# Token-major router logits, shorter VectorE routing chain, and what fills TensorE meanwhile, in a two-block transformer kernel on one core

## What is computed

```python
h2 = rmsnorm_2(x, norm2_w[layer])
x = x + hier_moe(h2, ...)            # 4 groups x 8 experts

p_group = softmax(x32 @ wg + bg)
pg, g_sel = lax.top_k(p_group, 1)
e_in = take_along_axis(e_logits, g_sel)[:, 0]
top_v, top_i = lax.top_k(e_in, 2)
gates = softmax(top_v) * pg
ids = g_sel * 8 + top_i
order = argsort(ids);  xs = xf[order // 2];  sizes = bincount(ids)
hg, hu = ragged_dot(xs, w_gate, sizes), ragged_dot(xs, w_up, sizes)
ys = ragged_dot(silu(hg) * hu, w_down, sizes) * gates
y = segment_sum(ys, tok)
```

## Time and profile before

| | |
|---|---|
| median of 3 runs | 1033.57 us (1033.43 to 1033.9) |
| profiled execution | 1033.82 us, span 1031.9 us |
| PE busy | 1010.1 us (98%), 5626 records |
| weight loads busy (PEld) | 873.2 us (85%) |
| DVE busy | 846.8 us (82%) |
| ACT busy | 706.1 us (68%) |
| DMA queues | 253.59 MB, mean 246 GB/s |
| granted clock | 0.998 of full speed |

### The profile page before, as it was taken

How to read it: one execution, slowest core, us unless ns; L and a number is a source line. 1 busy time by engine, 2 the same in 40 slices (tenths; PEclk the granted TensorE clock), 3 DMA queues, 4 the chain that set the end, 5 groups by cost and what they waited for, 6 DMA issues and landing times.

```text
span 1031.9 us, 15025 instructions
## 1 busy us (share of the span) xinstructions
PE 1010.1 (98%) x5626; PEld 873.2 (85%) x5626; DVE 846.8 (82%) x1044; ACT 706.1 (68%) x859; POOL 40.8 (4%) x44
## 2 busy tenths in 40 slices
PE   7999999999999999999999999999999999999997
PEld 6788999999989888999878788888888888888885
DVE  5855876766677877898869799999999999999987
ACT  5664655555565756576454688888888888888874
POOL 2001000000000110101020100000000000000000
PEclk9999999999999999999999999999999999999999
DMA  9734447474725455352215899999999999999971
GB/s 344 276 123 143 164 165 235 138 236 139 231 83 169 163 166 167 123 164 83 82 34 204 325 362 372 368 367 364 383 354 375 365 374 360 384 364 373 364 300 44
DMA packets 82709, 253.59 MB, mean 246 GB/s; under 512 B 4160, under 2 KB 42176, under 8 KB 62656
## 3 DMA queue, kind: packets, MB, share of 16 engines
q1 hardware_dynamic: 82624, 252.50, 67.9%
HBM read 251.44 MB, written 1.05 MB: 245 GB/s over the span
## 4 chain that ended last, share of the span: by engine, by line
PE 42%; DVE 3%; ACT 2%; issue 2%; DMA 1%; DVEq 0%; POOLq 0%; POOL 0%; ACTq 0%
PE bank L2020 13%; PE bank L2022 13%; PE bank L2021 13%; PE bank L2521 1%; DMA raw<-in_exp_w_down 1%; DVE WL L1080 1%; PE bank L2561 1%; ACT WH L541 1%; PE bank L2480 0%; PE bank L2489 0%; ACT MXH L923 0%; DVE MXL L1627 0%; PE bank L2593 0%; PE bank L2594 0%; ACT CV L918 0%
## 5 line engine op out<-in xcount | busy, mean ns | idle before, releaser
L1080 DVE TENSOR_TENSOR WL<-raw,WH 128x2048 fp32r<-128x2048 f32 x230 | 524.5, 2302 | 89.7 <-ACT WH L541 86.6
L541 ACT ACTIVATE WH<-raw 128x2048 fp32r<-128x2048 f32 x231 | 440.6, 1914 | 83.9 <-PE bank L2022 72.3
L2020 PE MATMUL bank<-WH,MXH 128*128 128x512 f32 x552 | 218.1, 395 | 0.7 <-DVE WL L1080 0.6
L2021 PE MATMUL bank<-WL,MXH 128*128 128x512 f32 x552 | 215.2, 390 | 0.0
L2022 PE MATMUL bank<-WH,MXL 128*128 128x512 f32 x552 | 215.2, 390 | 0.0
L2020 PE MATMUL bank<-HTH,WH 128*128 128x256 f32 x576 | 165.0, 286 | 1.2 <-DVE HTL L1103 1.2
L2021 PE MATMUL bank<-HTL,WH 128*128 128x256 f32 x576 | 162.9, 283 | 0.0
L2022 PE MATMUL bank<-HTH,WL 128*128 128x256 f32 x576 | 162.9, 283 | 0.0
L2020 PE MATMUL bank<-WH,HTH 128*128 128x512 f32 x400 | 159.6, 399 | 2.1 <-DVE WL L1127 1.0
L2021 PE MATMUL bank<-WL,HTH 128*128 128x512 f32 x400 | 155.8, 390 | 0.0
L2020 PEld LDWEIGHTS bank<-WH,MXH 128*128 128x128 f32 x552 | 103.7, 188 | 29.6 <-issue 8.5
(11 more groups left out here) (411 smaller groups left out, 1079.1 us busy)
## 6 DMA issues: line engine op xcount, KB each, us to landing
raw<-in_exp_w_up SPq DMA_DIRECT2D x52, 1024.0 KB, 7.4
raw<-in_exp_w_gate SPq DMA_DIRECT2D x52, 1024.0 KB, 7.4
raw<-in_exp_w_down SPq DMA_DIRECT2D x52, 1024.0 KB, 7.3
raw<-in_w_in SPq DMA_DIRECT2D x34, 1024.0 KB, 5.3
raw<-in_w_up SPq DMA_DIRECT2D x22, 1024.0 KB, 5.3
raw<-in_w_down SPq DMA_DIRECT2D x11, 1024.0 KB, 5.2
raw<-in_w_out SPq DMA_DIRECT2D x8, 1024.0 KB, 5.1
raw<-in_w_o SPq DMA_DIRECT2D x4, 1024.0 KB, 5.7
```

What stands on the lines that cost most here:

```text
L541: e.activation(WH[i % HL][:, :], raw[i % RAW][:, :], ACT.Copy).then_inc(a_wh, 1)
L1080: e.tensor_tensor(l, r, h.bitcast(F32), ALU.subtract).then_inc(v_wl, 1)
L2020: e.matmul(out_, ah, bh, start=start, stop=False, skip_group_check=skip)
L2021: e.matmul(out_, ah, bl, start=False, stop=False, skip_group_check=skip)
```

## The change

All in the stage between the last projection and the first unit.

- **Logits.** The transposed X stays float32 in the buffer BIG, one eviction each: three by ScalarE, the last by VectorE. It is now the stationary operand, and the 36 unsplit router columns move: 4 products for each part (c, t), into one bank for each token tile (`LGB`). The router's split, the low parts, ScalarE's eviction and `small_turn` are gone.
- **Best two.** Two instructions MAX and two MAX_INDEX give the eight largest of `el` and their places; one cast adds 100, and two comparisons with the codes give the one-hots.
- **Counts.** TensorE sums both token tiles in PSUM (32 columns), and adds tile 0's counts to tile 1's ranks. VectorE's prefix sum reads PSUM.
- **Tiles.** A round is one instruction with an accumulator output (`next_limit`), with three masks ready ahead; `first` counts the experts whose prefix sum is zero.
- **Slots.** `place(t)`: two multiply-and-reduce instructions for each token tile, right ahead of that tile's SEL.
- **Order.** `rows_low(1, 0)` goes behind the routing's sum MM, `rows_low(1, 1)` behind the first half of SEL; TensorE waits for each token tile's low rows apart. ScalarE's `rows_high(1, 0)` goes ahead of two evictions. The mean is one instruction behind the squares.
- **Filling.** `warm` 20 and 36 become 13 and 18.
- **ScalarE** splits piece NP+3 behind its gathered rows, no longer ahead of them.

```diff
-        xcols = [[v[PI["we", 1, 0] % HL][:, 0:4 * S].rearrange("p (k s) -> p k s", k=4) for v in (WH, WL)],
-                 [v[:, 0:4, :] for v in (HTH, HTL)]]
+        xcols = [big(1024 * c, 4, S) for c in range(2)]
...
-            e.activation(wsh[:, 0:288], wr_norm, ACT.Copy).then_inc(a_whs, 1)
...
             x_columns(0, 1)
             half_squares(1, 0)
+            rows_high(1, 0)
             x_columns(1, 0)
-            x_columns(1, 1)
             half_squares(1, 1)
-            rows_high(1, 0)
             rows_high(1, 1)
-            e.wait_ge(p_sp, 2)
-            e.activation(TMP[0:36, 1, 0:256], bank[4][0:36, 0:256], ACT.Copy).then_inc(a_sptv, 1)
...
             split(NP + 2)
-            split(NP + 3)
...
             for k in range(0, 8, 2):
                 gathered(k, 1)
+            split(NP + 3)
...
-            e.tensor_tensor(wsl[:, 0:288], wr_norm, wsh[:, 0:288].bitcast(F32), ALU.subtract).then_inc(v_wsl, 1)
...
-            top1(el, 32, const("iota", 32, 4), m1_, oh1)
             after()
-            e.scalar_tensor_tensor(out=el, in0=oh1, scalar=-2e30, in1=el, op0=ALU.mult,
-                                   op1=ALU.add).then_inc(own.up(), 1)
-            top1(el, 32, const("iota", 32, 4), m2_, oh2)
+            for t in range(T):
+                e.max(top8[:, t, :], el[:, t, :]).then_inc(own.up(), 1)
+            for t in range(T):
+                e.wait_ge(own.sem, own.n - 1)
+                e.max_index(idx8[:, t, :], top8[:, t, :], el[:, t, :]).then_inc(own.up(), 1)
+            after()
+            e.tensor_scalar(idxf, idx8[:, :, 0:2], 100.0, None, ALU.add).then_inc(own.up(), 1)
...
+            def next_limit(b):
+                e.scalar_tensor_tensor(out=FL.rearrange("p a b -> p (a b)")[:, 0:33], in0=tested[b - 1],
+                                       scalar=lim[:, b - 1:b], in1=cnt, op0=ALU.is_le, op1=ALU.mult,
+                                       accum_out=lim[:, b:b + 1]).then_inc(own.up(), 1)
...
-            for b in range(1, NT):
-                at, to = lim[:, b - 1:b], lim[:, b:b + 1]
-                after()
-                e.scalar_tensor_tensor(out=t1, in0=inc, scalar=at, in1=inc, op0=ALU.is_le,
-                                       op1=ALU.mult).then_inc(own.up(), 1)
...
+            def place(t):
                 after()
+                for i, (ohx, px) in enumerate(((oh1, pos), (oh2, pos2))):
+                    e.tensor_tensor_reduce(US[:, 32 * i:32 * i + 32], ohx[:, t, :], rank[:, t, :], 1.0, 0.0, ALU.mult,
+                                           ALU.add, px[:, t:t + 1]).then_inc(own.up(), 1)
...
+            def logits(c, t):
+                e.wait_ge(*((v_xtl, 1) if c and t else (a_xth, X_COLS[c, t])))
+                for i in range(4):
+                    k = 36 * (4 * c + i)
+                    m = e.matmul(bank[LGB[t]][:, 0:36], xcols[c][:, i, t * 128:(t + 1) * 128], wr_norm[:, k:k + 36],
+                                 start=(c == 0 and i == 0), stop=(c == 1 and i == 3))
...
-            warm(20, 0)
+            logits(1, 0).then_inc(p_sp, 1)
+            logits(1, 1).then_inc(p_sp, 1)
+            warm(13, 0)
...
-            warm(36, 0)
-            e.wait_ge(v_rl, 4)
+            warm(18, 0)
             for t in range(T):
+                e.wait_ge(v_rl, V_RL["low", 1, t])
                 e.wait_ge(v_sel, t + 1)
```

More of the change, by code:

```diff
@@ L121 @@
 V_ROUTE = numbered(["ge2", "mm", "dm", "first", "units", "gates"])
+V_RL = numbered([("low", 0, 0), ("low", 0, 1), ("low", 1, 0), ("low", 1, 1)])
 A_ROUTE = numbered(["ge2", "dm"])
-P_ROUTE = numbered(["counts", "gates"])
+P_ROUTE = numbered(["counts", "ranks", "gates"])
 HROW = numbered(["ffn", "n1"])
@@ L1653, in first_largest @@
             def first_largest(vals, n, iot, mval):
-                eq, idx = (topq, topi) if n == 32 else (topq[:, :, 0:n], topi)
+                eq, idx = topq, topi
                 after()
@@ L1690, in vector @@
-            rows_low(1, 1)
+            e.tensor_tensor(dm, top8[:, :, 1], top8[:, :, 0], ALU.subtract).then_inc(v_route, 1)
+            rows_low(1, 0)
+            counts = bank[6][:, 0:32]
             e.wait_ge(p_route, P_ROUTE["counts"])
-            e.reduce_sum(cnt, bank[6][:, 0:64].rearrange("p (t b) -> p b t", t=T), AX).then_inc(own.up(), 1)
-            e.tensor_copy(CR, bank[6][:, 0:128].rearrange("p (a b) -> p a b", a=4)).then_inc(own.up(), 1)
+            e.tensor_copy(cnt[:, 0:32], counts).then_inc(own.up(), 1)
@@ new lines, in vector @@
+            for b in range(1, 4):
+                e.scalar_tensor_tensor(out=tested[b], in0=inc, scalar=LEAST_AT[b], in1=inc, op0=ALU.is_gt,
+                                       op1=ALU.mult).then_inc(own.up(), 1)
+                if b == 1:
+                    e.wait_ge(own.sem, own.n - 1)
+                    e.tensor_copy(first, at_first).then_inc(v_route, 1)
+            e.wait_ge(own.sem, own.n - 2)
+            next_limit(2)
+            e.tensor_tensor(off, inc[:, 0:32], cnt[:, 0:32], ALU.subtract).then_inc(own.up(), 1)
@@ L1739, in vector @@
                 for t in range(T):
-                    after()
+                    if half == 0:
+                        place(t)
                     e.tensor_scalar(SEL[:, t, hs], iota[:, hs], pos[:, t:t + 1], None, ALU.is_equal).then_inc(own.up(), 1)
@@ L1748, in vector @@
                     m.then_inc(v_sel, 1)
-            e.tensor_tensor(inc, off, cnt, ALU.add).then_inc(own.up(), 1)
-            o4, i4 = (bc(v.unsqueeze(2), P, 32, NT) for v in (off, inc))
+                else:
+                    rows_low(1, 1)
+            e.tensor_tensor(off, off, t1, ALU.add).then_inc(own.up(), 1)
+            after()
+            e.tensor_tensor(inc[:, 0:32], off, cnt[:, 0:32], ALU.add).then_inc(own.up(), 1)
+            o4, i4 = (bc(v.unsqueeze(2), P, 32, NT) for v in (off, inc[:, 0:32]))
             lo, hi = (bc(const(n, NT).unsqueeze(1), P, 32, NT) for n in ("lo", "hi"))
@@ L2449, in turn_x @@
                 transpose4(2 * c + t, X[:, t, c * 512:(c + 1) * 512]).then_inc(p_xt, 1)
-            def logits(c, begin, end):
-                wh, wl = (v[:, 0:288].rearrange("p (k n) -> p k n", k=8) for v in (wsh, wsl))
-                xh, xl = xcols[c]
-                e.wait_ge(v_wsl, 2)
-                e.wait_ge(v_xtl, X_COLS[c, 1])
-                for i in range(begin, end):
-                    m = three(bank[4][0:36, 0:256], wh[:, 4 * c + i, :], wl[:, 4 * c + i, :], xh[:, i, :], xl[:, i, :],
-                              c == 0 and i == 0, c == 1 and i == 3)
+            def logits(c, t):
[4 more added lines that the diff above has]
+                                 start=(c == 0 and i == 0), stop=(c == 1 and i == 3))
                 return m
```

114 lines of the change are left out of this document (52 added, 62 removed).

## The result

| | before | after |
|---|---|---|
| median | 1033.72 us (4 runs, 1033.43 to 1033.9) | 1027.63 us (4 runs, 1025.94 to 1027.88) |
| profiled execution | 1033.82, span 1031.9 | 1027.49, span 1025.7 |
| granted clock, mean | 0.998 | 0.997 |
| DVE busy | 846.8 us | 840.8 us |

A forecast was written before the change was run, and what follows sets the result against it. TensorE was taken to lead, VectorE's small instructions setting when the units start; 1.8 + 1.4 + 3.6 - 0.1 = 6.7, taken as 6.6, from 1033.82 gave 1027.2 us, range 1025.8 to 1029.7.

The forecast's parts named there:

- Counts to SEL: VectorE's chain from the counts' arrival to SEL: 4.1 us instead of 7.74, gain 3.6 us.
- Accumulator reads charged nothing: VectorE's instructions with accumulator output: the read is hidden, no charge; upper bound 0.08 us for each of five, 0.4 us.
- Logits: From the projection's last product to the scaled logits: gain 1.8 us, bounds 1.3 and 2.1.
- Best two: VectorE's choice of two experts by MAX and MAX_INDEX: 1.6 us instead of 3.05, gain 1.4 us.
- ScalarE's split: ScalarE before the gathering's evictions: first split ends at 551.8; with the second still in front, TensorE would stand 2.9 us.
- Two PSUM sources: VectorE's prefix sum and rank addition reading PSUM: no charge, against 0.13 us together by the skill's rule.
- the filling ahead of the counts: TensorE's 13 products before the counts: 26 records in 2.9 us, then idle 0.5 us and not late.
- my rival: The clock falls around the shortened filling, through longer idle time, slowing the gathering by 7.7 us: 1036.3 us; chance 0.04.
- for steps rounded short: Allowance on the summed handover gain for an in-order chain: 6.7 us taken as 6.6.
- the chain is shorter than I count: Rival before the gathering: the filling then binds, ending at 547.0, at most 1.1 us more gain, 1026.1 us; chance 0.08.
- The transfers set the pace: Rival in the expert stage: only the first issue's 3.0 us move would arrive, 1030.8 us; chance 0.05.
- Late handover: Rival at the gathering: ScalarE or VectorE late; with late evictions TensorE stands 2.9 us, 1030.1 us; chance 0.10.

The follow-up runs named there:

- e9_rounds: Changed kernel with the tile limits found as before, by four rounds of four instructions, and 28 filling products behind the counts instead of 18: 1029.59 us, ratio 0.996.
- e0_again: The changed kernel run again without any edit, as the measure for other runs: 1026.15 us (5 runs), ratio 0.9933, clock 1.00 throughout its profile.
- e7_reductions: Changed kernel with the best two found as before, by reductions and comparisons, and 20 filling products ahead of the counts instead of 13: 1027.92 us, ratio 0.9942.
- e4_before_fill: Kernel before the change with only its filling cut, 13 and 18 products in place of 20 and 36: 1035.12 us (10 runs), ratio 1.0014.
- e2_warm6: Changed kernel with the first filling cut to 6 products instead of 13: 1027.05 us, ratio 0.9938.
- e6: Changed kernel with 16 additional unread products in the logits' stretch, in two versions, 36 or 128 columns each: 1033.76 us and 1030.01 us.
- e6_twice36: Changed kernel with 16 additional unread products of 36 columns each in the logits' stretch: 1033.76 us (10 runs), ratio 0.9997.
- e3_split_ahead: Changed kernel with ScalarE splitting piece NP+3 ahead of the gathered rows again, as before the change: 1028.95 us, ratio 0.9952.
- e8_low_early: Changed kernel with VectorE's low rows of the third part moved from behind MM to behind the second mean: 1026.74 us, ratio 0.9929.
- e1_wide: Changed kernel with the logits' 16 products moving 128 columns instead of 36, the further columns never read: 1027.12 us, ratio 0.9935.
- e5_fill36: Changed kernel with 36 filling products behind the counts, as before, in place of 18: 1029.42 us, ratio 0.9958.
- e6_twice128: Changed kernel with 16 additional unread products of 128 columns each in the logits' stretch: 1030.01 us (6 runs), ratio 0.9969.

## Why the prediction was right, and where it was wrong

**Right, by its steps.** *Counts to SEL*: 4.1 predicted, 3.90 measured, and e9_rounds puts 2.3 us of the gain on the rounds and 0.7 on what stands between them. One entry of that sum is misread: `place(0)` is two reductions, not four, and with their reads it takes 0.36 us where 0.45 was charged. *Accumulator reads charged nothing*: the limit L1687 shows 0.25 us, its read starts 0.18 us later and takes 0.08, and the next instruction without a wait (543.78) starts with the read. The Trainium skill's rule that such an instruction is two (VectorE: DVE Perf Modes, Two Vector instructions with no wait between them) is seen in the rows; as serial steps they would have been wrong, as the earlier trace rows had shown. *Logits*: gain 1.8 predicted; from the projection's last product to the second tile's scaled logits it takes 6.87 us before (540.41) and 5.02 in e0_again (538.30), 1.85 less. *Best two*: gain 1.4 predicted, 1.55 measured, between the scaled logits and the low rows (4.40 and 2.85 us) and in e7_reductions' median; MAX8 and FIND_INDEX8 with their loads, 0.69 us from the first MAX8 to the cast, lie by the row that I had taken as nearest, and not by the scan of 0.49. *ScalarE's split*: the transfer landed 5.0 us after its issue (5.1 predicted), the split ended at 552.1 (551.8). With the second split ahead the prediction let TensorE stand 2.9 us; it stood 2.0, because the second piece landed sooner than in the kernel before, so that the 2.8 us of the median is near 2.9 partly by chance. *Handover*: no wait inside the gathering. *Two PSUM sources*: 0.21 and 0.22 us, as the nearest rows had it.

**Wrong: the filling ahead of the counts.** The step "TensorE is idle 0.5 us, and not late", behind a filling of 26 records in 2.9 us, failed in the profiled execution, and with it came a sign that the prediction itself had named as wrong, a granted clock below 1 between 538 and 560. The filling took 4.52 us, most of it at the clock's lower level, the counts started 1.2 us later against the projection than in e0_again (9.16 and 7.94 us), and what followed moved with them. At the upper level the step is right in kind, 3.15 us in e0_again with 0.24 us of idle time, which shows how thin the margin was. I had looked for the clock's fall in idle time alone: my rival decides "from where the change makes an idle time that is longer than that one". e4_before_fill shows that way to exist, and e2_warm6 shows it for a shorter idle time behind narrow products. But what happened in the changed kernel was the other condition that the rival named in passing, "the logits' columns shrink from 256 to 36": the clock fell with TensorE busy throughout, and the two versions of e6, which differ in nothing but columns, point there. The rival's price, 1036.3, was also for a fall that lasts through the gathering; this one was over before it and cost 0.87 us at the handover. The Trainium skill (TensorE: Matmul & The Clock Gate, Part 1) lists half rate as the state of an idle or cold array and full rate as that of a busy one; here a stretch without idle time got to half rate (8.00 of 8.00 us busy at 0.50 in e6_twice36), and the row decides.

**Wrong by less: the sum.** With the clock up the handover moves by 7.24 us: 1.85 by the logits, 1.55 by the best two, 3.84 by counts to SEL, which I had at 1.8, 1.4 and 3.6, less 0.1 for a stall that didn't come and 0.1 "for steps rounded short", which had no ground. Each is small, and all have one sign. The rival "the chain is shorter than I count" has the direction, and its 1026.1 lies by the measured 1026.15 and 1026.37; but its condition, that the filling then binds, wasn't met: TensorE was idle for 0.54 us behind the filling in e0_again. So the hit of the profiled execution is a chain that is 0.6 us shorter than counted, and a fall of the clock that takes 0.87 us of it back at the handover. How many of the other executions had such a fall isn't shown; the four executions of after and the ten later ones overlap (1025.94 to 1027.88, 1025.46 to 1028.41).

**The other rivals.** *The transfers set the pace*: would have left 3.0 us; all shifts arrive in full, to 6.2 us of the span, and SP's queue still waits 307.0 us for VectorE. *Late handover*: not in the changed kernel; it appears in e3_split_ahead and e6_twice36, in the place that was named.

**Left open.** In the nine profiles with the short stretch of narrow products the clock fell there in two (after and e8_low_early), with the same TensorE instructions up to there. That these two falls have the cause that the versions of e6 show is inferred: e1_wide, which should have shown it, met no fall to undo. What decides that from one execution to the next isn't shown. Nor do the means of the clock explain the spread of 1.7 to 2.7 us between executions of the changed kernel on one chip. The logits' form was not undone by itself; its 1.85 us are read from the traces alone, and so is what counts to SEL gained beyond the rounds and the interleaving, some 0.9 us. No version tried beats the changed kernel.

## What to carry to other kernels

Where one engine's chain of small instructions sets a handover, take it apart as a chain: count what waits on the one before, put the independent instructions between, and carry along what stood behind the old length (fillings, the order of the evicting engine), or much of the gain stays there: here 3.2 of 7.24 us in e5_fill36 and 2.8 of 7.5 in e3_split_ahead. Look at the granted clock of each stretch that the change makes of narrow products, even where TensorE is never idle, and of each idle time behind a filling that gets shorter. And compare two profiles of one kernel before explaining a microsecond: here the handover differs by 0.87 us between two profiles of the same instructions.

## What the runs showed of the hardware that was not expected

- The granted clock went from 1.00 to 0.50 with TensorE busy in every microsecond, behind products that moved 36 columns; with half of the products at 128 columns it stayed at 1.00 (e6_twice36, e6_twice128). It came back during the filling's products of 128 columns (e6_twice36).
- The clock can fall behind an idle time rather than in it: after 1.80 us of it, with the narrow logits ahead, TensorE resumed at 1.00 and had 0.66 in the five busy microseconds from 543 (e2_warm6). After 1.83 us without them it stayed at 1.00 (e4_before_fill).
- Eight largest of 32 columns: 0.29 us for two MAX8 in a row; a search for their places 0.18 us and its load 0.07 to 0.09.
